# Gating tokens 0 to 255 inside steps 9 to 15 of attention, and turning the context tiles between the first products

## The reference, cut to what matters

```python
# first block: the six vectors of modulation are columns of one product with w_ada
sh1, sc1, gt1, sh2, sc2, gt2 = split(silu(c) @ w_ada + b_ada)
csh1, csc1, ...              = split(silu(c_ctx) @ w_ada + b_ada)
hc = rmsnorm(ctx, g_pre_mix) * (1 + csc1) + csh1     # 256 tokens
hx = rmsnorm(x,   g_pre_mix) * (1 + sc1)  + sh1      # 512 tokens
# both go into products with w_in, then a gated linear attention, a convolution, an FFN

# second block
gates = sigmoid(z[..., o4:] + b_gate)                # g_pool, g_attn: 1024 columns each
a = pool_mixer(...)
b = swa_sink_attention(q, k, v, sinks)               # 16 heads of 64, blocks of 128 queries, 256 keys
x = x + (g_pool * a + g_attn * b) @ w_out
# then an FFN of 2816
```

## Time and profile before

| | us |
|---|---|
| median of 3 runs | 1478.83 |
| the three runs | 1479.35, 1478.83, 1474.08 |
| the profiled execution | 1479.79 |
| its span, first to last instruction | 1478.0 |
| TensorE busy | 1394.6 |
| VectorE busy | 890.1 |
| GpSimd busy | 835.2 |
| ScalarE busy | 399.8 |

### The profile page before, as it was taken

The page is one execution under the profiler, slowest core; times in us unless marked ns, Lnnn a source line. Parts: engine busy times, 40 slices in busy tenths (PEclk is TensorE's granted clock), DMA queues, the critical chain, the costliest instruction groups (busy, mean ns, idle before and its releaser), DMA issues.

```text
span 1478.0 us, 19684 instructions
## 1 busy us (share of the span) xinstructions
PE 1394.6 (94%) x6923; PEld 1124.7 (76%) x6923; DVE 890.1 (60%) x1269; ACT 399.8 (27%) x757; POOL 835.2 (57%) x651
## 2 busy tenths in 40 slices
PE   6898889989799999999998999999699999999998
PEld 4677667878478888888877888767488888888887
DVE  5579678774566666660018688743674888887000
ACT  3430323332332222220003203255522333232000
POOL 1233333434566666667775577432166777777765
PEclk9899989989889999999998999999999999999999
DMA  9359312111123333333332233211033333333332
GB/s 356 120 185 303 82 43 58 58 44 57 57 58 100 99 98 89 97 92 97 100 96 72 82 90 97 75 43 55 18 99 87 96 89 99 99 99 87 95 93 82
DMA packets 224459, 142.05 MB, mean 96 GB/s; under 512 B 5611, under 2 KB 211088, under 8 KB 224400
## 3 DMA queue, kind: packets, MB, share of 16 engines
q1 hardware_dynamic: 223509, 140.65, 31.7%
q10 hardware_dynamic: 891, 0.58, 0.1%
HBM read 139.12 MB, written 2.10 MB: 96 GB/s over the span
## 4 chain that ended last, share of the span: by engine, by line
PE 80%; DVE 13%; ACT 2%; issue 2%; DMA 1%; POOL 1%; SPq 0%; DVEq 0%; POOLq 0%
PE ps L544 24%; PE ps L546 23%; PE ps L545 23%; DVE ada_acc L1743 2%; DVE g_z L1844 1%; PE ps L833 1%; DVE norm_acc L1656 1%; PE ps L1074 1%; DMA v_tok<-in_w_ada 1%; PE ps L1090 1%; PE ps L1103 1%; ACT h_hi L1177 1%; PE ps L629 1%; DVE SS L1926 1%; DVE xT L2094 1%
## 5 line engine op out<-in xcount | busy, mean ns | idle before, releaser
L507 POOL TENSOR_TENSOR w_lo<-raw,w_hi 128x1024 fp32r<-128x1024 f32 x213 | 535.5, 2514 | 17.8
L544 PE MATMUL ps<-h_hi,w_hi 128*128 128x512 f32 x1064 | 428.9, 403 | 12.4 <-DVE h_lo L1677 6.9
L546 PE MATMUL ps<-h_hi,w_lo 128*128 128x512 f32 x1064 | 420.3, 395 | 0.0
L545 PE MATMUL ps<-h_lo,w_hi 128*128 128x512 f32 x1064 | 420.2, 395 | 0.0
L503 POOL TENSOR_TENSOR w_hi<-raw,cst 128x16 fp32r<-128x16 f32 x213 | 62.5, 293 | 595.9 <-PE ps L546 533.8
L544 PEld LDWEIGHTS ps<-h_hi,w_hi 128*128 128x128 f32 x1064 | 203.3, 191 | 64.8 <-issue 18.7
L546 PEld LDWEIGHTS ps<-h_hi,w_lo 128*128 128x128 f32 x1064 | 203.1, 191 | 44.0
L545 PEld LDWEIGHTS ps<-h_lo,w_hi 128*128 128x128 f32 x1064 | 203.7, 191 | 40.2
L504 POOL TENSOR_SCALAR w_hi<-raw 128x1008 fp32r<-128x1008 f32 x213 | 231.2, 1086 | 0.0
L2015 DVE SCALAR_TENSOR_TENSOR f_acc<-ps,par,f_acc 128x441 f32<-128x441 f32 (+2 forms) x176 | 122.3, 695 | 50.2 <-ACT f_acc L1177 27.9
L544 PE MATMUL ps<-f_hi,w_hi 128*128 128x512 f32 x352 | 138.3, 393 | 0.2 <-POOL w_lo L507 0.2
(11 more groups left out here) (291 smaller groups left out, 1956.7 us busy)
## 6 DMA issues: line engine op xcount, KB each, us to landing
raw<-in_w_up SPq DMA_DIRECT2D x88, 512.0 KB, 3.7
raw<-in_w_in SPq DMA_DIRECT2D x59, 512.0 KB, 3.8
raw<-in_w_down SPq DMA_DIRECT2D x32, 512.0 KB, 3.6
v_tok<-in_w_ada SPq DMA_DIRECT2D x18, 512.0 KB, 5.8
ada_first<-in_w_ada SPq DMA_DIRECT2D x8, 1024.0 KB, 10.0
raw<-in_w_out SPq DMA_DIRECT2D x16, 512.0 KB, 3.6
ada<-in_w_ada SPq DMA_DIRECT2D x14, 512.0 KB, 5.4
raw<-in_w_down SPq DMA_DIRECT2D x16, 384.0 KB, 3.3
```

Source lines behind the costliest of these rows:

```text
L507: pool.tensor_tensor(w_lo[:, slot % 2, :], raw[:, slot, :], w_hi[:, slot % 2, :].bitcast(F32), ALU.subtract).then_inc(S("lo_split"), 1)
L544: nc.tensor.matmul(dst, lhs_hi, rhs_hi, start=first, stop=False)
L545: nc.tensor.matmul(dst, lhs_hi, rhs_lo, start=False, stop=False)
L546: return nc.tensor.matmul(dst, lhs_lo, rhs_hi, start=False, stop=last)
```

## The change

The context tiles are turned in two pairs inside `two_units`, ahead of its places 2 and 3; row 4 goes from place 3 to 4, row 5 from place 5 to 6. In attention, tokens 0 to 255 of the tiles are gated one tile at a time: tiles 0 and 1 in step 9, 2 and 3 in step 10, 4 in step 11, 5 in 13, 6 in 14, 7 in 15. Tokens 256 to 511 of tiles 0 to 3 are gated in step 14 by one pair of instructions over four tiles; of tiles 4 to 7, tokens 256 to 383 are gated behind the loop, ahead of the last sums and reciprocals, and tokens 384 to 511 behind the last outputs. The low parts of tiles 0 and 1 move ahead of the last outputs. On ScalarE the high parts of tiles 0 and 1 move into step 15, behind its exponentials and ahead of its copies of the turned probabilities.

```diff
@@ -686,19 +686,20 @@
         ada_pair(5)
         turn_row(2)
         turn_row(3)
-        turn_inputs(range(10, 14))
 
         def between_products(at):
 
             if at == 2:
+                turn_inputs(range(10, 12))
                 ada_pair(6)
             elif at == 3:
+                turn_inputs(range(12, 14))
+            elif at == 4:
                 turn_row(4)
-            elif at == 4:
                 pe.wait_ge(S("ctx_turned"), 4)
                 ada_pair(7)
                 sum_squares(1, TC)
-            elif at == 5:
+            elif at == 6:
                 turn_row(5)
             elif at == 8:
                 spread(1, TC, "rinv_ready")
@@ -1591,8 +1592,16 @@
                 act.wait_ge(S("o_scaled"), half - 1)
             activate(share[:, half % 2, :], ps[:, share_bank(half), :], ACT.Copy).then_inc(S("share_copied"), 1)
 
+        def y2_high(k):
+
+            act.wait_ge(S("y2_sum"), k // 4 + 1)
+            activate(y2_hi[:, k, :], qT[:, k, :], ACT.Copy).then_inc(S("y2_hi_ready"), 1)
+
         for s in range(STEPS):
             probs(s)
+            if s == STEPS - 1:
+                y2_high(0)
+                y2_high(1)
             if s and s % 2 == 0:
                 copy_shares(s // 2 - 1)
             copy_probs(s)
@@ -1600,10 +1609,8 @@
                 copy_shares(2 * BLOCKS - 1)
             if s and gate_done_in(s - 1):
                 gate(gate_done_in(s - 1))
-        for k in range(KT):
-            if k % 4 == 0:
-                act.wait_ge(S("y2_sum"), k // 4 + 1)
-            activate(y2_hi[:, k, :], qT[:, k, :], ACT.Copy).then_inc(S("y2_hi_ready"), 1)
+        for k in range(2, KT):
+            y2_high(k)
 
         load_sqrt(1)
         for m in range(KT):
@@ -2248,32 +2255,30 @@
             elif s >= 2 and gate_done_in(s - 2) in (6, 7):
                 pool_gated(gate_done_in(s - 2))
 
-            if s >= STEPS - 3:
-                if s == STEPS - 3:
-                    dve.wait_ge(S("pool_gated"), 8)
-                    dve.wait_ge(S("o_scaled"), 2 * BLOCKS - 2)
-                for k in ((0, 1, 2, 3), (4, 5), (6,))[s - STEPS + 3]:
-                    dve.wait_ge(S("gate_tanh"), 9 + k)
-                    order.done(attention_gated(k, slice(0, T - P)))
+            for k in {9: (0, 1), 10: (2, 3), 11: (4,), 13: (5,), 14: (6,), 15: (7,)}.get(s, ()):
+                dve.wait_ge(S("gate_tanh"), 9 + k)
+                dve.wait_ge(S("o_scaled"), 4)
+                dve.wait_ge(S("pool_gated"), 8)
+                order.done(attention_gated(slice(k, k + 1), slice(0, 2 * P)))
+            if s == STEPS - 2:
+                order.wait()
+                dve.wait_ge(S("o_scaled"), 2 * BLOCKS - 1)
+                attention_gated(slice(0, 4), slice(2 * P, T)).then_inc(S("y2_sum"), 1)
+        order.wait()
+        order.done(attention_gated(slice(4, KT), slice(2 * P, 3 * P)))
         shares(2 * BLOCKS - 1)
-        dve.wait_ge(S("gate_tanh"), 16)
-        order.done(attention_gated(KT - 1, slice(0, T - P)))
-
-        def last_gated(half):
-
-            dve.wait_ge(S("o_scaled"), 2 * BLOCKS - 1 + half)
-            attention_gated(slice(4 * half, 4 * half + 4), slice(T - P, T)).then_inc(S("y2_sum"), 1)
 
         def y2_low(k):
 
             dve.wait_ge(S("y2_hi_ready"), k + 1)
             vec.tensor_tensor(y2_lo[:, k, :], qT[:, k, :], y2_hi[:, k, :].bitcast(F32), ALU.subtract).then_inc(S("y2_ready"), 1)
 
-        last_gated(0)
-        outputs(2 * BLOCKS - 1)
         y2_low(0)
         y2_low(1)
-        last_gated(1)
+        outputs(2 * BLOCKS - 1)
+        dve.wait_ge(S("o_scaled"), 2 * BLOCKS)
+        order.wait()
+        attention_gated(slice(4, KT), slice(3 * P, T)).then_inc(S("y2_sum"), 1)
         for k in range(2, KT):
             y2_low(k)
```

## The result

| kernel | median of its runs, us | ratio to the kernel before, 95% interval |
|---|---|---|
| before (19 runs) | 1478.06 | |
| changed (19 runs) | 1482.34 | 1.0033, 1.0025 to 1.0041 |

The change makes the kernel slower by 0.33%, 4.9 us (3.7 to 6.1). The profiled execution took 1484.18 us (span 1482.4), 4.4 more than that of before. I had forecast 1.0 less.

A forecast was written before the change was run, and what follows sets the result against it. TensorE, 80% of the chain of waits, was taken as the bound, losing time where it waits or runs at the lower clock. End -3.0 plus start +2.0 gave -1.0 us: 1477.8 from a 1478.83 median, range 1471.5 to 1483.

The forecast's parts named there:

- the term for the start's clock: Start: clock may fall in the new 3.9 us wait before row 4, costing +0.6 to +1.6 us; taken at +0.8.
- The order: Start: row 5, turned behind six products' matmuls, comes 1.2 to 1.5 us later and delays product six; +1.2 us.
- the rival "slower": Start: clock falls before row 4, stays 0.50 over 12 matmuls, 2.4 us more, 3.6 in all; 1479.4 to 1480.4; chance 0.20.
- the 1.9 us wait ahead of product six: Start: with row 5 turned at 52.1, product six can't start before 54.35, so TensorE waits 1.9 us.
- (a): Attention steps 9 to 11: five gating pairs of 0.80 us fit into VectorE's idle time; costed at nothing.
- (b): Step 13: one gating pair instead of four, 3.44 us less; TensorE's wait 1.6 us in place of 5.07.
- (c): After step 13's wait the clock stays up: spread and scores about 1.0+1.1 us, not 1.9+2.0, another 1.85 us.
- (d): VectorE's added work before the last reciprocals gives back 2.4 of 5.3 us; last spread at 1055.4, not 1058.31 (-2.9).
- (e): Last spread to the output product's third tile takes 4.8 us instead of 6.26 with the clock up; another -1.4 us.
- (f): Clock may fall behind the 3.2 us wait before the last spread; taken at +1.3, leaving the end gaining 3.0 us.
- The shared port: Step 11: VectorE's sum beside GpSimd's instructions, taken at 0; as rival, caught by the long one, +1.1, 1478.9, chance 0.05.
- The rival that the clock holds at both places: Start and end: no clock fall behind the 3.9 and 3.2 us waits; -4.3+1.2 = -3.1 us, 1475.7; chance 0.15.

The follow-up runs named there:

- experiment 4: Kernel before with only the start's new order, plus unread matmuls filling TensorE's waits there (15, 6, 28, 14): 1480.82 us, ratio 1.0018.
- experiment 10: Changed kernel whole, both edits, with unread matmuls in TensorE's waits at the start (15, 6, 28, 14) and ahead of the last spread (26): 1475.51 us, ratio 0.9983.
- experiment 1: Kernel before with only the start's edit (context tiles turned in pairs, rows 4 and 5 each later): 1485.43 us, ratio 1.0050.
- experiment 3: Kernel before with only the start's edit, but row 5 back at place 5; attention as before: 1481.22 us, ratio 1.0027.
- experiment 5: Kernel before with only row 4 moved to place 4 and row 5 to place 6, turns still ahead of the products: 1481.20 us, ratio 1.0016.
- experiment 7: Kernel before with the gating edit, 26 unread matmuls ahead of the last spread and 44 in the old order's 5.58 us wait: 1476.79 us, ratio 0.9981.
- experiment 9: Kernel before with both edits, row 5 back at place 5, unread matmuls in the waits at start (15, 6, 28) and end (26): 1474.76 us, ratio 0.9977.

## Why the prediction was wrong

**The step that failed** is the term for the start's clock, "I take +0.8", in a start that "loses 2.0 (bounds 1.0 and 3.6)". That start lost 7.7 us at the context's scaling, and 6.4 of them are the clock's: three falls, where I had priced one. Against the kernel before, by TensorE's rows, with experiment 4 (same order, clock up) taking the order's part out:

| stretch | later than before, us | order (experiment 4) | clock |
|---|---|---|---|
| to row 4's turn (46.61 to 48.93) | 2.32 | 0.16 | 2.16 |
| row 4's to row 5's turn (4.20 to 7.99) | 3.79 | 1.10 | 2.69 |
| row 5's turn to the context's scaling (5.80 to 7.39) | 1.59 | 0.00 | 1.59 |
| sum | 7.70 | 1.26 | 6.44 |

- The order was forecast at +1.2: measured 1.26 in experiment 4 and 1.52 in experiment 10. "Row 5 stands behind them, 1.2 to 1.5 later, at 52.1" and "TensorE waits 1.9" held (52.07; 1.79).
- *The middle row* is the rival "slower": the clock falls in the wait before row 4 and stays down, 2.4 us. It measured 2.69, but the near agreement is luck. The rival counted only the twelve matmuls of the products, at 0.2 each. In the changed kernel seven of the twelve ran slow (the clock was back before 56; in experiment 1 it was not), and row 4's turn, the ada pair (1.94 us, 1.07 in experiment 4) and the sum of squares (1.02, 0.61), which I had left out, paid as well. I gave this rival a chance of 0.20, although the kernel before had stayed at 0.50 through 5 us of full work, and took +0.8.
- *The first row* I had not seen at all. I let the first two products run "in what was TensorE's wait" and asked what they save, not what they leave. The wait of 5.58 us became one of 2.03 with thin work behind it, and the fall came some 3 us earlier (the granted clock was 0.69 in 35 to 36; before, 0.74 in 38 to 39), over products and turns that now feed ScalarE. Hence row 4's copy at 48.51, not "about 46.4". Against experiment 3, whose trace lacks this fall and has no filling matmuls, it is 48.93-47.10 = 1.83.
- *The third row*: I had forecast the 1.9 us wait ahead of product six and given it no fall. Experiment 5 shows that fall by itself.

With 6.4 in place of 0.8 the sum is -3.0+1.2+6.4 = +4.6 us; the profiled executions lie 4.4 apart. That this comes so near is partly luck, as the stretches between vary by more (below).

**What held.** The end, step by step, with the shift of 7.19 taken out (my "0.133 us for each 128 columns" is one instruction's; a pair takes twice that, 0.27, which is what the costs of the pairs used, and 0.80 and 2.4 measured 0.79 and 2.40): (a) the five pairs of 256 columns in steps 9 to 11 cost nothing (the first score products, the spread of 1031.09 and the score products of 1038.89 are shifted by 7.21, 7.18 and 7.19). (b) TensorE's wait 1.61, forecast 1.6. (c) Spread and scores 1.09 and 1.14, forecast 1.0 and 1.1. (d) The last spread at 1055.38, forecast 1055.4; the wait ahead of it 3.20, forecast 3.2. (e) To the third tile with the clock up 4.87, forecast 4.8. (f) The clock fell; it cost 6.42-4.87 = 1.55, taken at 1.3. The shared port: the tiny sum took 0.58 beside GpSimd's instruction of 1035.46, the spread behind it was not late, as forecast.

The rival that the clock holds at both places had -3.1 us. That is what experiment 10 built: -2.5 (-4.1 to -0.9).

**Still open.** How often each of the three falls comes. The first one is in the trace of the changed kernel and of experiment 1 and not in that of experiment 3 behind the same 2.03 us wait; each trace is one execution. The runs of experiment 1 say only that the start loses 7.4 us (5.3 to 9.5), beside the traces' 7.0 and 7.7 at the context's scaling. The rest of the kernel varies too: from that scaling to the score products of step 12, a stretch that the kernels differing in the start alone share line by line, it took 982.3 us in the kernel before and 981.3, 978.6, 980.8 and 981.4 in experiments 1, 3, 4 and 5. So one trace places a loss, and only the many runs size it for the whole kernel.

## What to carry to other kernels

When work is moved into a long wait of TensorE, list the waits that are left, and what runs behind each: a harmless slow stretch, beside an engine that is late anyway, can be exchanged for one on the path. Price such a wait at itself alone and at itself plus a fall of the clock (here 1.6 to 2.7 us each on the path), give both a chance, and sum over the waits. Count in a fall everything that TensorE runs in it, the small matmuls too. Filling every such wait with matmuls that nobody reads is a cheap test of that, and it made this change faster than the kernel before; no filled kernel was shown to beat the gating edit alone. Filling only one wait moved the fall to the next in experiment 7.

## What was not expected of the hardware

- Waits of 1.79, 2.03 and 2.26 us each had a fall behind them in some execution; in experiment 5 the 1.79 us came in a stretch otherwise busy. None of them is sure to: 2.03 had none in experiment 3, the same 1.79 none in experiment 1, and 1.86 us ahead of the output product none in the kernel before:

```profile
60.13 0.50 PE L544 MATMUL ps<-h_hi,w_hi 128*128 128x512 f32 x1 [1.79 <-DVE h_lo L1678]
```
```profile
1062.13 0.47 PE L544 MATMUL ps<-y_hi,w_hi 128*128 128x512 f32 x1 [1.86 <-DVE y_lo L2270]
```

- In experiment 9 the clock fell shortly before 50 without a wait over 0.7 us in the eight microseconds ahead.
- In experiment 1 TensorE stayed at 1.2 GHz through eight microseconds of full work (8.00 of 8.00 busy in 49 to 57).
